# Forgetting attention: the causal mask added by VectorE in the score bank, in place of a bf16 mask product on TensorE

## What is computed

```python
def forgetting_attention(q, k, v, f_logit):
    ...
    F = jnp.cumsum(jax.nn.log_sigmoid(f_logit.astype(jnp.float32)), axis=1).transpose(0, 2, 1)
    ...
    def block(args):
        q_blk, F_blk, pos_blk = args
        s = jnp.einsum('bhqd,bshd->bhqs', q_blk, k, preferred_element_type=jnp.float32)
        s = s + F_blk[..., None] - F[:, :, None, :]
        s = jnp.where(pos_blk[:, None] >= k_pos[None, :], s, -jnp.inf)
        p = jax.nn.softmax(s, axis=-1).astype(v.dtype)
        return jnp.einsum('bhqs,bshd->bqhd', p, v)
```

## Time and profile before

| | |
|---|---|
| Time, median of 3 runs (lowest, highest) | 1825.17 us (1825.15, 1825.67) |
| Span of the profiled execution | 1826.2 us |
| TensorE busy | 1791.9 us, 98% |
| VectorE busy | 1174.9 us, 64% |
| ScalarE busy | 740.4 us, 41% |
| GpSimd busy | 1314.0 us, 72% |
| First and last start of the 32 mask products (L2553) | 1044.2, 1155.8 us |

### The profile page before, as it was taken

How to read it: one execution, slowest core, us unless ns; L and a number is a source line. 1 busy time by engine, 2 the same in 40 slices (tenths; PEclk the granted TensorE clock), 3 DMA queues, 4 the chain that set the end, 5 groups by cost and what they waited for, 6 DMA issues and landing times.

```text
span 1826.2 us, 28390 instructions
## 1 busy us (share of the span) xinstructions
PE 1791.9 (98%) x10212; PEld 1525.8 (84%) x10212; DVE 1174.9 (64%) x1771; ACT 740.4 (41%) x1385; POOL 1314.0 (72%) x1188
## 2 busy tenths in 40 slices
PE   9999999999999999999999999999999998999998
PEld 7788888878878799998888877798876778999886
DVE  7976674149974798877017767574454189888631
ACT  5521111137762466652024267553423255666001
POOL 8986666667777798877667865453772689888775
PEclk9999999999999999999999999999999999999999
DMA  7022223232223323234223311201321222323421
GB/s 279 1 94 90 92 92 138 92 127 82 79 72 113 139 93 116 93 120 178 95 93 104 113 50 46 70 26 47 116 92 47 92 99 87 116 98 111 166 100 69
DMA packets 26014, 179.36 MB, mean 98 GB/s; under 512 B 2864, under 2 KB 2992, under 8 KB 6960
## 3 DMA queue, kind: packets, MB, share of 16 engines
q1 hardware_dynamic: 24176, 168.31, 25.9%
q10 hardware_dynamic: 1728, 9.58, 1.4%
HBM read 171.58 MB, written 6.29 MB: 97 GB/s over the span
## 4 chain that ended last, share of the span: by engine, by line
PE 84%; DVE 7%; ACT 3%; POOL 3%; issue 2%; DMA 1%; ACTq 0%; DVEq 0%; POOLq 0%
PE bank L484 12%; PE bank L486 12%; PE bank L485 12%; PE bank L1432 6%; PE bank L1434 6%; PE bank L1433 6%; PE bank L1904 2%; PE bank L1902 2%; PE bank L1903 2%; PE bank L522 1%; PE bank L523 1%; PE bank L524 1%; POOL weights_lo L762 1%; DVE temps L1628 1%; PE bank L2307 1%
## 5 line engine op out<-in xcount | busy, mean ns | idle before, releaser
L376 POOL TENSOR_TENSOR weights_lo<-raw_weights,weights_hi 128x512 fp32r<-128x512 f32 (+4 forms) x400 | 540.8, 1352 | 39.8 <-ACT weights_hi L395 7.2
L374 POOL TENSOR_SCALAR weights_hi<-raw_weights 128x512 fp32r<-128x512 f32 (+4 forms) x376 | 263.1, 700 | 317.5 <-PE bank L486 169.6
L484 PE MATMUL bank<-x_hi,weights_hi 128*128 128x512 f32 x688 | 271.5, 395 | 0.2 <-POOL weights_lo L376 0.2
L486 PE MATMUL bank<-x_lo,weights_hi 128*128 128x512 f32 x688 | 267.9, 389 | 0.0
L485 PE MATMUL bank<-x_hi,weights_lo 128*128 128x512 f32 x688 | 267.8, 389 | 0.0
L484 PEld LDWEIGHTS bank<-x_hi,weights_hi 128*128 128x128 f32 x688 | 129.2, 188 | 27.8 <-POOL weights_lo L376 0.8
L485 PEld LDWEIGHTS bank<-x_hi,weights_lo 128*128 128x128 f32 x688 | 129.3, 188 | 27.1 <-issue 1.0
L486 PEld LDWEIGHTS bank<-x_lo,weights_hi 128*128 128x128 f32 x688 | 129.2, 188 | 27.2
L1434 PE MATMUL bank<-x_lo,weights_hi 128*128 128x256 f32 x432 | 122.2, 283 | 0.0
L1474 POOL TENSOR_TENSOR weights_lo<-temps,weights_hi 128x512 fp32r<-128x512 f32 x72 | 107.7, 1515 | 4.6 <-ACT weights_hi L1511 4.6
L1474 POOL TENSOR_TENSOR weights_lo<-raw_weights,weights_hi 128x512 fp32r<-128x512 f32 x72 | 98.5, 1373 | 12.7 <-ACT weights_hi L1511 12.4
(11 more groups left out here) (587 smaller groups left out, 5201.0 us busy)
## 6 DMA issues: line engine op xcount, KB each, us to landing
raw_weights<-in_ffn_seven SPq DMA_DIRECT2D x36, 1024.0 KB, 4.7
raw_weights<-in_a_ug SPq DMA_DIRECT2D x16, 1024.0 KB, 4.8
raw_weights<-in_b_in SPq DMA_DIRECT2D x12, 1024.0 KB, 4.8
raw_weights<-in_ffn_down SPq DMA_DIRECT2D x12, 1024.0 KB, 4.8
raw_weights<-in_ffn_down SPq DMA_DIRECT2D x7, 1408.0 KB, 6.2
raw_weights<-in_a_out SPq DMA_DIRECT2D x8, 1024.0 KB, 4.7
raw_weights<-in_ffn_up SPq DMA_DIRECT2D x8, 1024.0 KB, 4.8
raw_weights<-in_b_out SPq DMA_DIRECT2D x8, 768.0 KB, 4.2
```

The costliest lines, as they stand in the source:

```text
L374: nc.gpsimd.tensor_scalar(hi, raw, 1.0, 0.0, ALU.mult, ALU.add).then_inc(S("units_hi"), 1)
L376: nc.gpsimd.tensor_tensor(lo, raw, hi.bitcast(F32), ALU.subtract).then_inc(units_ready, 1)
L484: nc.tensor.matmul(ps, wh, xh[:, k, :], start=k == 0, stop=False)
L486: last = nc.tensor.matmul(ps, wh, xl[:, k, :], start=False, stop=k == last_k)
```

## The change

The mask product goes from TensorE, with its two bf16 tiles, ScalarE's two copies into them, and the semaphore `mask_b`. VectorE adds the f32 mask to the own block of the score bank, in place, when the scores are done, and its maximum waits for that addition (`fx_masked`). VectorE waits once, ahead of the loop, for the mask from GpSimd.

```diff
-        IDENT_B = place("ident_b", ZAT + 28, [P], BF16)
-        CAUSAL_B = place("causal_b", ZAT + 28.25, [P], BF16)
...
-            nc.scalar.activation(IDENT_B[:, :], IDENT[:, :], ACT.Copy).then_inc(S("mask_b"), 1)
-            act.wait_ge(*due("causal", 2))
-            nc.scalar.activation(CAUSAL_B[:, :], CM, ACT.Copy).then_inc(S("mask_b"), 1)
...
         def pe_fox(pe):
             pe.wait_ge(*due("fk", PFQ.rounds - 1))
-            pe.wait_ge(*due("mask_b", 2))
...
                     nc.tensor.matmul(ps[:, 0:n], F_SEL[:, h % 2, qt * P:n], F_K[:, 0:n], start=True, stop=False)
-                    nc.tensor.matmul(ps[:, n - P:n], IDENT_B[:, :], CAUSAL_B[:, :], start=False, stop=False)
...
         def dve_fox(dve, step):
             MXC, SUMC = SC[:, 0:32], SC[:, 32:64]
+            dve.wait_ge(*due("causal", 2))
...
                     n = (qt + 1) * P
+                    own_block = score_bank(i)[:, n - P:n]
                     dve.wait_ge(*due("fx_s", i + 1))
+                    nc.vector.tensor_tensor(own_block, own_block, CM, ALU.add).then_inc(S("fx_masked"), 1)
+                    dve.wait_ge(*due("fx_masked", i + 1))
                     nc.vector.reduce_max(MXC[:, i:i + 1], score_bank(i)[:, 0:n], axis=AX.X, negate=True).then_inc(S("fx_nm"), 1)
```

More of the change, by code:

```diff
@@ L166 @@
     *(_members(kind, ("fx", FOXH * TOK), ("ma", MH * TOK)) for kind in ("s", "nm", "e", "p", "t", "pt")),
-    [("b_xc_lo", KB), ("row_sel", 3), ("f_rows", 1), ("gb_split", 4), ("go_with_q", TOK), ("column_half", 1)], [("b_xc_hi", KB), ("row_ones", 3), ("mask_b", 2), ("f_queries", 2)],
+    [("b_xc_lo", KB), ("row_sel", 3), ("f_rows", 1), ("gb_split", 4), ("go_with_q", TOK), ("column_half", 1)], [("b_xc_hi", KB), ("row_ones", 3), ("f_queries", 2), ("fx_masked", FOXH * TOK)],
     [("beta_tanh", 1), ("a_exp", 1), ("rows_exp", 1)],
```

## The result

The changed kernel takes 1832.54 us (median of 6 runs, 1830.60 to 1833.93) beside 1825.47 for the kernel before (6 runs, 1825.15 to 1827.19): a ratio of 1.0033 [1.0023, 1.0043]. It is slower by some 6 to 7 us. The profiled run took 1833.93, the longest of the six, with a span of 1832.2, so its details are those of a dear execution.

The account below looks back on a forecast made before the run. TensorE was taken to bound the kernel, with VectorE and ScalarE leading in three loop stretches; additions cost 3.77 us, removing the mask product saves 0.98, net +2.8: 1828.0 us, range 1825.4 to 1830.1.

Parts of the forecast that it names:

- Rival 2: Each addition is stretched by GpSimd or the bank to 0.43 to 0.5 us: 1829.1 to 1829.9 us, chance 0.08.
- A: Attention loop, maximum of step 3 to scores of step 12: VectorE and ScalarE lead, five additions of 0.33 us count.
- B: Attention loop, step 13's maximum to the transposes of step 18: VectorE and ScalarE lead, three additions of 0.33 us count.
- C: Attention loop, step 21's maximum to the transposes of step 26: three additions of 0.33 us count; TensorE leads behind it.
- row 5: Step 5's normalized row from ScalarE: the wait of TensorE's transposes for it should grow from 0.8 to over 2 us.
- row 9: Step 9's normalized row from ScalarE: TensorE's wait for it should be new or longer.
- Row 18: Step 18's normalized row from ScalarE: a new or longer TensorE wait, its transposes later by about 2.2 us.
- rival 4: TensorE's stalls in the loop lengthen and the clock falls, losing 1.7 us: 1829.7 us, chance 0.04.
- 0.8 us stall: TensorE's longest wait for a normalized row in the loop before, forecast to become over 2 us.
- Rival 3: VectorE bounds the whole loop, so all 29 additions from step 3 on are paid: +9.2 us, 1834.4 us, chance 0.03.

Follow-up runs that it names:

- e1: The kernel before without its mask product and nothing in its place, scores unmasked: 1825.08 us, ratio 0.9993.
- e9: The changed kernel again, unaltered, for a second profile and more runs: 1832.60 us, ratio 1.0028.
- e3: The changed kernel with GpSimd's subtraction for the low weight parts of two projections replaced by a memset of zero: 1824.85 us, ratio 0.9992.
- e4: The kernel before with GpSimd's subtraction for the low weight parts of two projections replaced by a memset of zero: 1823.19 us, ratio 0.9988.
- e8: The changed kernel with the next head's query subtraction moved from the end of the step to right behind the maximum: 1826.03 us, ratio 1.0004.

## Why the prediction was wrong

**Right: the price of one addition.** 0.301 us was forecast, 0.293 to 0.294 came in the runs with the full width, and the maximum follows 0.03 behind it (1057.49 + 0.30 to 1057.82). The addition, with one SBUF input, was not stretched by GpSimd: none took over 0.30, those that began inside a split of GpSimd included. Rival 2 falls, and so far the Trainium skill (SBUF — State Buffer, Who interferes with whom) held.

**Right: what the mask product costs TensorE.** Timeline of TensorE at a step of 256 columns, the changed kernel, for step 13 in the earlier trace rows:

```profile
1073.54 0.28 PE L2546 MATMUL bank<-fox_f_rows,fox_f_selected 128*128 128x256 f32 x1
1073.65 0.28 PE L2547 MATMUL bank<-fox_k_even,fox_q_even 128*128 128x256 f32 x1
1073.77 0.28 PE L2548 MATMUL bank<-fox_k_even,fox_q_even 128*128 128x256 f32 x1
```

From first to last score product 0.23, before 0.36. The price of 0.12 to 0.13 holds. The Trainium skill's 134 cycles for 128 columns (TensorE: Matmul & The Clock Gate, Back-to-back issue gap), an estimate of 56 ns, is less than half of what these rows show the product to cost among its neighbours. How much of it the loop gets back was forecast at 0.98; e1 shows 0.5 in one profile.

**Right: where the additions go, and the direction.** They are pieces of the chain in A and B (in C the chain view follows TensorE, up to 1145); TensorE's wait for row 5 passed 2 us (2.51, at 1065.99), and that for row 9 grew from 0.54 to 2.77. The other two waits came one row earlier than forecast, at the rows 17 and 25 (2.50, 2.47) instead of 18 and 26. Row 18 has three blocks to transpose, row 17 two:

```profile
1115.76 0.44 PE L2557 MATMUL bank<-ident,fox_p 128*128 128x128 f32 x2 [2.50 <-ACT fox_p L2667]
...
1119.96 0.52 PE L2557 MATMUL bank<-ident,fox_p 128*128 128x128 f32 x3
```

The scores of step 13 came 4.5 late rather than 1.1 to 1.3, and the transposes of row 18 came 7.4 late (1119.96 - 1042.56 beside 1114.00 - 1044.04) rather than 2.2. Without GpSimd's subtraction the change costs 1.45 us of the loop, with the query rests moved 3.2, beside the forecast 2.8. So the additions' own price was about right; no run shows it apart from everything else.

**Wrong: VectorE's other operations were held at their durations of before.** This is the step that failed. The sum has no term for them. In the first profile the rests and taps on the path took 3.8 us more than before and two other taps 0.3 less; the slow products add 3.2 to 3.4. I asked of the addition alone whether GpSimd stretches it. The chain that I followed had instructions with two SBUF inputs, the query and key rests and the taps, and the change delays VectorE against GpSimd. The same instruction of the same step took 1.67 us when GpSimd's subtraction had begun and 0.69 when it had not (the changed kernel and e9). In all profiles a rest that begins inside GpSimd's subtraction or rounding ends 0.52 to 0.59 us after GpSimd's instruction ends, wherever in it it began. The other way round, a rounding that begins inside a rest ends 0.5 to 0.6 after the rest. The Trainium skill (SBUF — State Buffer, Who interferes with whom) says that a VectorE instruction with two SBUF inputs contends with a GpSimd instruction that reads SBUF, and calls the port pair that they share an exclusive lock; these ends agree with it. e3 and e4 show that without GpSimd's subtraction most of the excess goes; e8, that with one of the rests off the chain most of it goes. The earlier trace rows had a hint: L2347 at 920 and 900 between others at their plain cost says that encounters are common, and the same trace has the odd queries' rest at 0.99 us at 1076.72 and at 0.69 at 1105.94.

**Wrong: the clock was held at 1.00 (rival 4).** It got a chance of 0.04 and a price of 1.7 us. I had reasoned from the earlier trace rows that a lower clock comes in this kernel, and from 1.00 in the loop that no lower clock follows the 0.8 us stall. My own forecast made that stall over 2 us, so the cover for "the clock stays" was gone by my own sum. In the changed kernel the waits of 2.77 and 2.50 us were followed by slow products, those of 2.51 and 2.47 by none; in e9 those of 2.54 and 2.48 were, and that of 2.51 wasn't; e8's 2.44 wasn't either. No kernel whose longest wait was under 2.1 us had any. At 0.20 for each of 16 products, the dips cost some 3.2 us in the first profile and at most 2.2 in e9, where those at 1066 lay in a stretch that VectorE led. In all profiles together 8 of the 12 waits of 2.1 us or more were followed by slow products.

**Rival 3** (VectorE bounds the whole loop, 1834.4) comes nearest as a number and is not what happened: TensorE leads behind C as before (that part became 0.26 shorter), and with the same VectorE work e3's loop is 110.5.

What stays open: how the excess divides between encounters and clock in the typical run. The two profiles of the changed kernel, 120.8 and 117.7, are of one execution each, and the clock falls because stalls grow, which the encounters lengthen, so the two can't be added as if independent. That an encounter is one instruction held up by the other rests on where they end, on e9's pair and on e3 and e4; nothing here measured the two instructions by themselves. How the cost divides between the additions' own time and what they set off differs by pair (1.45 and 3.2 us of loop). Why some stalls over 2.1 us are followed by the lower clock and others aren't was not settled.

## What to carry to other kernels

Price what a change delays as well as what it adds: list the instructions behind it on its engine that have a conflict of their own, and ask what each costs if it falls on the neighbour's work. When your own sum lengthens a stall of a nearly full TensorE to over 2 us, count the slow clock behind it as part of the forecast and not as a rival of 4 in 100; here it followed 8 of 12 such stalls. An operation that may be stretched belongs in an engine's idle time, not on the chain between two engines.

## What the runs showed of the hardware

- One fp32 subtraction of 64x512 on VectorE, with both inputs in SBUF, took 0.69 us alone and 1.67 when it began 0.48 us into GpSimd's subtraction of 128x512, and 1.72 when it began 0.11 us into one. Begun inside such a subtraction, or inside GpSimd's rounding (one input), it ended 0.52 to 0.59 us after GpSimd's instruction in every profile: an encounter costs what is left of GpSimd's instruction, less about 0.15.
- GpSimd's subtraction took 1.29 us alone and 1.60 where it had begun 0.45 before the end of a VectorE tap (changed kernel, 1076.35 beside the tap until 1076.80); its rounding took 0.62 alone and 0.99 when it began 0.18 us into a rest (e3, 1103.65). Its memset beside a rest left both at their time (e3 at 1090.67: 0.68 of the even keys' rest, and 0.53 of the memset).
- Two executions of one kernel, with the same order on every engine, differed in which of these met: loops of 120.8 and 117.7 us.
- Of the 12 waits of TensorE's transposes of 2.1 to 2.8 us in these loops, 8 were followed by products at the lower clock (0.43 us apart instead of 0.23), in six profiles; those of up to 1.8 us never were.
- An addition of 128x128 in a bank took 293 ns, one of 128x8 169 ns: most of its price is fixed.
